# A hybrid streaming encoder layer on eight cores: the DMA transposes of x moved into the second layer's down projection, their loads made steps of their own, and the two normalisation rows loaded independently

## What is computed

```python
h = LN1(ALPHA * x + 0.5 * SwiGLU_1(x))          # silu(x @ wg) * (x @ wu) @ wd
z = h @ w_in                                    # q | k | v | x_lru | gate_lru
A = chunked sliding-window attention with sinks (8 heads of 64, window 128, chunk 64)
B = causal conv (width 4) + RG-LRU (width 512), times a GeLU gate
h = LN2(ALPHA * h + concat(A, B) @ w_out)
h = LN3(ALPHA * h + 0.5 * SwiGLU_2(h))
y = h + sigmoid(h @ w_ple_gate) * (p @ w_ple)
```

## Time and profile before

| | us |
|---|---|
| median of three runs | 6040.25 |
| the three runs | 6040.25, 6051.3, 5299.7 |
| the profiled execution | 5315.45 |
| span of its slowest core (core 0) | 5313.9 |
| spans of the other cores | 5268.2 to 5295.5 |
| TensorE busy, core 0 | 4887.3 |
| VectorE (DVE) busy | 3012.6 |
| ScalarE (ACT) busy | 1729.1 |
| GpSimd (POOL) busy | 598.6 |

### The profile page before, as it was taken

The page is one execution under the profiler, slowest core; times in us unless marked ns, Lnnn a source line. Parts: engine busy times, 40 slices in busy tenths (PEclk is TensorE's granted clock), DMA queues, the critical chain, the costliest instruction groups (busy, mean ns, idle before and its releaser), DMA issues.

```text
span 5313.9 us, 80104 instructions; the slowest of 8 cores (5268.2 to 5313.9 us)
## 1 busy us (share of the span) xinstructions
PE 4887.3 (92%) x24230; PEld 2285.9 (43%) x24711; DVE 3012.6 (57%) x4850; ACT 1729.1 (33%) x3749; POOL 598.6 (11%) x1069
## 2 busy tenths in 40 slices
PE   6796898999989999999998999999899999999978
PEld 3342343444444444444444444444444444444433
DVE  2355555655665556665655556565565656556664
ACT  1151532514233142332514234251423415142331
POOL 1011211001010010101001010100101011010110
PEclk8898999999999999999999999999999999999989
DMA  9859968585754757667575765747576574756554
GB/s 203 209 157 165 214 178 198 149 224 146 212 143 145 226 148 215 172 191 182 155 217 142 215 165 182 195 148 221 145 216 173 178 195 147 221 146 209 165 139 147
DMA packets 506193, 956.27 MB, mean 180 GB/s; under 512 B 269328, under 2 KB 278096, under 8 KB 505776
## 3 DMA queue, kind: packets, MB, share of 16 engines
q1 hardware_dynamic: 242064, 828.92, 49.9%
q0 software_dynamic: 31392, 64.50, 8.1%
q10 hardware_dynamic: 232320, 57.70, 8.0%
HBM read 880.76 MB, written 77.09 MB: 180 GB/s over the span
## 4 chain that ended last, share of the span: by engine, by line
PE 70%; DMA 12%; DVE 6%; issue 5%; ACT 4%; ACTq 1%; POOL 1%; SPq 0%; DVEq 0%; POOLq 0%
PE ps_all L346 69%; DMA actT<-xb 5%; DMA bring<-wbg 2%; ACT P L372 2%; DVE lnst L574 1%; DVE hbuf L389 1%; DMA wsb<-bring 1%; PE ps_all L350 1%; DMA pbuf<-p 1%; DVE ft L389 1%; ACTq L625 1%; DMA rope_c<-rope 1%; DMA bring<-wsb 1%; ACT Pb L372 1%; DVE am L992 1%
## 5 line engine op out<-in xcount | busy, mean ns | idle before, releaser
L346 PE MATMUL ps_all<-actT,bring 128*128 128x512 bf16 x11032 | 2527.2, 384 | 228.3 <-DVE ft L389 120.8
L346 PEld LDWEIGHTS ps_all<-actT,bring 128*128 128x128 bf16 x11264 | 1104.1, 99 | 1552.5 <-issue 294.3
L346 PE MATMUL ps_all<-bring,hid 128*128 128x512 bf16 x5491 | 1265.3, 381 | 33.8 <-DVE hbuf L389 8.9
L372 ACT ACTIVATE ft<-ps_all 128x512 f32<-128x512 f32 x748 | 426.1, 574 | 2068.9 <-PE ps_all L346 1867.2
L389 DVE SCALAR_TENSOR_TENSOR ft<-ft,ps_all 128x512 f32<-128x512 f32 x748 | 490.9, 656 | 816.0 <-ACT ft L372 789.9
L346 PEld LDWEIGHTS ps_all<-bring,hid 128*128 128x128 bf16 x5632 | 544.0, 98 | 654.8 <-issue 54.3
L389 DVE SCALAR_TENSOR_TENSOR hbuf<-hbuf,ps_all 128x512 f32<-128x512 f32 x384 | 247.7, 683 | 539.3 <-PE ps_all L346 539.3
L380 DVE TENSOR_TENSOR hid<-ft,ps_all 128x512 bf16<-128x512 f32 x704 | 480.0, 682 | 84.3 <-PE ps_all L346 52.9
L389 DVE SCALAR_TENSOR_TENSOR hbuf<-hbuf,lnst,gbuf 128x1024 f32<-128x1024 f32 x384 | 486.3, 1278 | 9.4 <-POOL lnst L579 8.1
L346 PE MATMUL ps_all<-actT,fring 128*128 128x512 bf16 x1624 | 391.4, 385 | 12.2 <-ACT P L372 8.4
L372 ACT ACTIVATE Pb<-P,aden 128x192 bf16<-128x192 f32 (+1 forms) x516 | 233.8, 453 | 143.0 <-DVE aden L1011 105.5
(11 more groups left out here) (126 smaller groups left out, 3224.4 us busy)
## 6 DMA issues: line engine op xcount, KB each, us to landing
bring<-wsb SPq DMA_DIRECT2D x970, 512.0 KB, 4.1
fring<-wsf SPq DMA_DIRECT2D x255, 512.0 KB, 5.0
bring<-wbg POOLq DMA_DIRECT2D x64, 512.0 KB, 15.3
wsb<-bring SPq DMA_DIRECT2D x64, 512.0 KB, 10.1
hbuf<-x SPq DMA_DIRECT2D x64, 512.0 KB, 7.1
y<-hbuf SPq DMA_DIRECT2D x64, 512.0 KB, 6.6
gbuf<-ln_g SPq DMA_DIRECT2D x48, 512.0 KB, 5.4
gbuf<-ln_b SPq DMA_DIRECT2D x48, 512.0 KB, 5.1
```

Source lines behind the costliest of these rows:

```text
L346: return P.op("pe", lambda e: e.matmul(out, lhsT, rhs, start=start, stop=stop), reads, writes, cost=(max(0.056, fsz(rhs) * 0.00042), 0.165 ...
L372: return P.op("act", lambda e: e.activation(out, in_, func, **kw), reads, writes, cost=acost(out, func))
```

## The change

Three things are changed.

- The `Tx` steps of tiles 2 to 15 get a further condition: the four transposes of tile t may be placed only after the steps (hf 0, block 1), (hf 0, block 3), (hf 0, block 5) and (hf 1, block 1), each with sub-tile 3, of the down projection of FFN 2 of tile t-2. That is the last backbone stage ahead of `up 1` of tile t. The planner also counts 1.2 us of ACT's time for each DMA transpose, where it had counted only its usual issue cost.
- The load of x two places on is no longer issued within the `Tx` step but is a step `xb` of its own, placed once the planner believes its buffer free, and the `Tx` step that needs it comes after it.
- The beta row of `gbuf` gets its own name and semaphore, `gb1`; its load no longer waits for that of the gamma row.

```diff
--- before.py
+++ after.py
@@ -584,7 +584,7 @@
                 (hn, mn, "gb"), (hn,))
 
         def c():
-            stt(hv[0:nt, :], hv[0:nt, :], rstd[0:nt, :], gbuf[0:nt, 1, :], ALU.mult, ALU.add, (hn, rn, "gb"), (hn,))
+            stt(hv[0:nt, :], hv[0:nt, :], rstd[0:nt, :], gbuf[0:nt, 1, :], ALU.mult, ALU.add, (hn, rn, "gb1"), (hn,))
 
         def d():
             return
@@ -600,7 +600,7 @@
 
         return [Step(("La",) + key, a, (hn,), (), src_after),
                 Step(("Lb",) + key, b, (hn, mn, "gb"), (), gbi=gname),
-                Step(("Lc",) + key, c, (hn, rn), ()),
+                Step(("Lc",) + key, c, (hn, rn, "gb1"), ()),
                 Step(("Ld",) + key, d, (hn,), ()),
                 Step(("Le",) + key, e_, (hn,), (), nbuf=True),
                 Step(("Lf",) + key, f, lambda: ("nb%d" % st["nb"],), lambda: a_sets(akey, s), (), nbank=0 if by_dma(akey) else 1,
@@ -624,6 +624,7 @@
             tn = a_name(akey, s)
             o_ = P.op("act", lambda e: e.dma_start_transpose(out=dst, in_=src[0:nt, :]), sname, (tn,), dsem="t" + tn,
                       nbytes=nt * D * 2)
+            P.free["act"] += 1.2
             o_.fin += 4.0
             return
         bk = take_bank()
@@ -653,7 +654,7 @@
         def load(gk=gk):
             gb_cur[0] = gk
             dma("sp", gbuf[:, 0, :], lng_d[gk[0]].partition_broadcast(128), (), ("gb",), "gb", nonc=True)
-            dma("sp", gbuf[:, 1, :], lnb_d[gk[0]].partition_broadcast(128), (), ("gb",), "gb", nonc=True)
+            dma("sp", gbuf[:, 1, :], lnb_d[gk[0]].partition_broadcast(128), (), ("gb1",), "gb1", nonc=True)
         aft = ()
         if i >= 1:
             aft = tuple(("Ld", m[0], m[1], s) for m in gb_members[gb_order[i - 1]] for s in range(geom(m[1])[1]))
@@ -799,6 +800,8 @@
             return nb16[i - 2], ("nb%d" % (i - 2),)
         return xb16[i % 2], ("xb%d" % (i % 2),)
 
+    xl_ = []
+
     def tx_steps():
         out = []
         for i, (t, s) in enumerate(xb_seq):
@@ -806,7 +809,7 @@
                 nt = geom(t)[2]
                 b, n = xb_of(i)
                 transpose_in(b, n, ak, s, nt, "act" if s % 2 else "dve")
-                if i not in (2, 3, 4):
+                if i not in (2, 3, 4) and not by_dma(ak):
                     i2 = (6, 5)[i] if i < 2 else i + 2
                     if i2 < len(xb_seq):
                         xb_load(i2)
@@ -814,8 +817,14 @@
             pre = ()
             if t < NP and t >= 2:
                 pre = (("Lf", 0, t - 1, 3),)
+                if i >= 2 and by_dma(("x", xb_seq[i - 2][0])):
+                    pre += (("xb", i),)
+                if by_dma(ak):
+                    pre += (("dn", 2, t - 2) + ((0, 1), (0, 3), (0, 5), (1, 1))[s] + (3,),)
             out.append(Step(("Tx", t, s), fn, xb_of(i)[1], lambda ak=ak, s=s: a_sets(ak, s), pre, nbank=0 if by_dma(ak) else 1,
                             aall=ak if s == 0 and t != SMP else None, aneed=ak if s else None))
+            if by_dma(ak) and i + 2 < len(xb_seq):
+                xl_.append(Step(("xb", i + 2), lambda i=i: xb_load(i + 2), (), xb_of(i + 2)[1], (("Tx", t, s),)))
         return out
 
     def xl_step(t, s):
@@ -1335,6 +1344,7 @@
     add(8, [Step(("kl",), lambda: dma("pool", cvb, ck_d, (), ("kfin",), "ck"), (), (),
                  (("vx", NP - 1),) if NP - 1 == RM else (("up", 1, 0, NF - 1, 1),))])
     add(5, tx_steps())
+    add(5, xl_)
     for t in ([0, SMP, 1] if NP > 1 else [0, SMP]):
         add(0, [xl_step(t, s) for s in range(geom(t)[1])])
     for t in mseq:
```

## The result

The changed kernel takes 5180.0 us (median of its four runs: 5175.02, 5177.15, 5182.85 and 5719.14). Against comparable runs of the kernel before the ratio is 0.9768, with a 95% interval of 0.9747 to 0.9789: 2.3% faster. Executions in which some cores show a lower granted clock are longer whatever the kernel (in the 5719.14 us one, four cores have 0.874 to 0.875 and the others 0.978 to 0.98); they, and with them the 6040.25 and 6051.3 us of before, are left out of every comparison here. The forecast was 5184 us, 2.5% under the profiled execution of before.

A forecast was written before the change was run, and what follows sets the result against it. TensorE, busy 92% of the span, was taken as the bound, so only its idle or lower-clock time could be won. 128.7 + 10 - 7 - 0 - 0 = 131.7 us off 5315.45 gave 5184 us, range 5130 to 5265.

The forecast's parts named there:

- step 5: Beta row's load on SyncE without its wait for the gamma row: taken as 0, since six weight buffers cover it.
- step 1: First input projections, tiles 4 to 15: moving late transposes and their loads removes TensorE's stalls, gain 128.7 us.
- the witness, tile 3: Tile 3's window: same instruction order, transposes landed early, 29.89 of 30 us TensorE work; taken to show late transposes the cause.
- The signs that I named: Expected in the changed profile: smaller chain entry and waits, fuller windows at clock 1.00, a tile about 300 us instead of 310.
- the lower clock: Matmuls after each idle stretch run at 1.2 GHz: 2.7 us lost in each of 12 tiles, 32.4 us.
- Step 2: Tile 2's transposes in the start, window 485 to 545 us: gain 10 us, bounds 0 and 37.
- Step 3: Moved transposes in the down projection: ACT issue cost 0.5 us per tile, 7 us for 14 tiles; DMA share 0.50.
- Step 4: Last transpose before the next up projection: some 15 us of matmuls cover a landing of 9 us, cost 0.
- Half comes back: Late transposes in the down projection stop attention, returning half the 10.7 us in 13 tiles: 5254 us, chance 0.18.
- bound anyway: Input projections keep a shorter wait from the chain of POOL, ACT and DVE, 7 of 10.7 us remaining: 5271 us, chance 0.10.
- the slower rival: Two `xb` buffers hold ACT in the down projection and the last transpose comes late: 5438 us at 24 us landing, chance 0.06.

The follow-up runs named there:

- c1: The changed kernel run again, unchanged, on the same chip as three other experiments: 5196.77 and 5213.26 us.
- a7: Kernel before with only the beta row on its own semaphore, planner told the old times so the order stays nearly the same: 5244.42 to 5253.35 us, ratio 0.9862.
- a4: Changed kernel with the beta row's load waiting behind the gamma row again: 5205.88 to 5225.32 us, ratio 0.9795.
- c2: Kernel before with the transposes of x three blocks of up 2 (some 10 us) later, beta row's wait kept: 5232.54 to 5245.38 us, ratio 0.9849.
- a6: Changed kernel with the four transposes later in the down projection, the last at its end: 5467.71 us in one execution.
- A: Transposes of x spread over the down projection; alone on the kernel before, loads still directly behind the transposes: 5241.87 us.
- B: Loads of x as steps of their own; alone on the kernel before, transposes still in the input projections: 5312.24 us.
- C: Beta row's load under its own name and semaphore; alone on the kernel before: 5254.5 and 5247.88 us.
- b1: Changed kernel with tile 2's x transposed by TensorE and the last prompt tile's state stores after its second LayerNorm: 5208.07 to 5227.81 us, ratio 0.981.

## Why the prediction was right, and where it wasn't

The time, 5184 against 5180.0, agrees better than the steps behind it deserve. Some of it is chance: the same kernel took 5196.77 and 5213.26 us in c1. The step that failed is step 5, the beta row, and with it the reason that step 1 gave for the late transposes.

*Step 5, the beta row: this step failed.* "I take 0 ... nothing below zero, since a wait is only dropped" looked for a wait of TensorE for `bring` and found none. The row's worth ran by another path: its wait held back the next loads, which then ran into ScalarE's transposes. Alone it gives 57 to 66 us in the middle, 1.4% of the kernel's time in a7. In the sum the error didn't show, because step 1 had already booked the same stalls. As a term of this sum, behind step 1, the 0 holds for the middle (a4); as a statement on the edit it was wrong, and it hid what step 1 was about.

*Step 1, the stalls of tiles 4 to 15: right in size for core 0, its cause half read.* I concluded from the witness, tile 3, that late transposes are the cause, which the runs bear out. Why they were late I put down to the DMA share of 1.06. The beta row alone, with the share still 1.06, and c2 show that it was mostly one meeting in the queues: three loads, held back by a wait on SyncE, issued in the same 1.3 us. The signs that I named came, but for two small ones: no `actT<-xb` in the chain, `ft` from 89.5 to 6.6 us (I had said under 15), GpSimd's waits for the transposes 2.3 us each (one of 6.2, where I had said under 5), a tile of core 0 down from 314.7 to 304.9 us in the mean of twelve, and one of the twelve windows at 28.70 us, where I had said over 29. The windows gave 94.5 of the 96.3 us. At equal work core 0's middle gained 129.7 us, where the step has 128.7: 100.7 of idle time for its 96.3, and 28.9 of busy time for the 32.4 that it put on the lower clock. The median core gained 96.4. The sum was made on the slowest core, and part of what made it the slowest was more stalls than the others had (`ft` 89.5 us against 61.6 to 70.6). It still gave the right time, since the time is that of the slowest core, and core 0's middle fell to that of the others (3646.2 us).

*Step 2, the start: sized too small for core 0.* I took 10 us of 0 to 37; 22.8 were gained on core 0, 18.9 in the median core and 7.6 there in c1. The start was short of DMA, as the step says, and the trace shows the price in kind: the window from 485 to 545 us went from 27.86 to 54.14 us of TensorE work, the next from 57.80 down to 38.37. The stall moved into the next window and got shorter.

*Step 3, the transposes' cost on ScalarE: 0 where I had 7.* TensorE's work in the window of the down projection rose from 54.23 to 56.81 us, and the middle of core 0 gained all that step 1 promised. The share of 0.50 that I had worked out for that window was 0.69; what else fell into it wasn't looked into. One reading in this step was wrong without touching the sum: the pair that took 6.94 us didn't have "a fourth" under way beside it. The transpose ahead of it had landed at 4342.94, before the second of the pair was issued at 4343.27.

*Step 4, the cover: right.* The list has no wait of TensorE for `actT<-xb`, and a6 shows what it costs without: 75.6 us in that wait alone.

*The rivals.* "Half comes back" and "bound anyway" are out, with eleven of the twelve windows at 29.84 of 30 and 56.81 of 58 us in the down projection. In the slower rival the landing time had to be 19.6 us; it was 4.8, and the four issues stood 9.4, 12.5 and 10.3 us apart, 21.9 from the first to the third, where I had 20. Its second half, a last transpose too late for the up projection, is what a6 shows where the cover is short; its first, ScalarE held for a buffer, no run shows.

The tail was not in the sum. On core 0 it took back 19.4 us (the wait of 22.91 us for `fring<-wsf`, where before had 6.62 at that place for DVE); in the median core it didn't change (424.9 and 424.2). That this met the gains beyond the forecast on the same core, 13 us in the start and 8 in the middle, and cancelled them, is luck.

## What to carry to other kernels

When a transfer is late, look at what every other queue issued in the same microsecond or two, and ask what held that back; the cure may be there. A DMA that waits for another one on an issuing engine bunches all that stand behind it, and no wait of the compute engine need show it. Try parts alone, and together, before adding them up: two edits that remove the same stall (A with B, and C) are worth it once, and A without B was worth half. Size a gain on all cores, not on the one that the page shows. And compare stages of two kernels at equal work of the engine that bounds them: a planner that shifts steps also shifts the marks.

## What was unexpected of the hardware

- A transpose's landing time hung on what was issued beside it more than on the share of the DMA engines. At a share of 1.06 over 24 us the pair landed 14.9 and 17.9 us after its issues when 1.5 MB were issued from SyncE within 1.3 us of the first; at the same share, with the beta row and the next weights issued 5.6 and 3.2 us ahead, the pair took 6.3 and 7.0. In a6, after and c2 the medians of all 56 are 4.2 to 5.4 us. What decides inside the queues, these runs don't show.
- DMA engines can be busy and move little. In the tail of the changed kernel the share is 0.98 at 40 GB/s, of which SyncE's queue has 85.9% for 0.27 MB and ScalarE's 11.6% for 0.52 MB, and ScalarE's queue is held 29.41 us by two transposes. Windows of that stretch, and the issue:

```profile
4950.00:4970.00 20.00, 15.98 (x60) 6.68 (x62) 8.89 (x12) 2.09 (x2) 1.09 (x1) 0.76 0.98 40
4970.00:4995.00 25.00, 2.09 (x7) 0.72 (x6) 9.05 (x15) 0.00 (x0) 5.36 (x10) 0.57 1.03 142
```

```profile
4955.35 29.41 ACTq L625 DMA_TRANSPOSE actT<-nb  x2
```

  The stores of 4 bytes per element ahead of it were the suspects, but with them moved behind it the wait of the slowest core stayed (23.76 us in b1). Its cause is open.
